# Weight tiles 576 bytes apart under moving rows 2112 bytes apart, 528 columns taken as 256 and 272, three raw buffers instead of four

## The chip, the core and the metric

The kernel runs on one core of one Trainium2 chip. The metric is the device time of one execution in microseconds, the median of the runs shown. Before the change three runs took 3562.27, 3562.84 and 3564.36 us.

## What is computed

The reference is a chain of two transformer-like blocks on one sequence of 512 tokens with 1024 features. The first block prepends 16 learned tokens (528 in all) and has two layers; each projects the normed sequence with one wide matrix, takes a sparse attention, a recurrent branch and a convolutional branch from it, merges the three through gates, and adds a gated feed-forward part:

```
for l in range(DEPTH):                      # 2 layers, T = 528
    n = rms_norm(h, mix_norm_g[l])
    proj = jnp.einsum("btd,de->bte", n, w_in[l])
    attn, rnn, cnv = ...                    # three branches of proj
    merged = g_attn * (attn @ w_o_attn[l]) + g_rnn * (rnn @ w_o_rnn[l]) + g_conv * (cnv @ w_o_conv[l])
    h = h + merged @ w_out[l]
    f = rms_norm(h, ffn_norm_g[l])
    h = h + (silu(f @ w_ffn_gate[l]) * (f @ w_ffn_up[l])) @ w_ffn_down[l]
return h[:, N_META:]                        # 512 tokens go on
```

The second block (feed-forward, neighbourhood attention beside a state-space branch, feed-forward, a gated product with a per-layer embedding, a last norm) works on the 512 tokens. All in float32. Most of the work is products of a float32 weight matrix with the sequence.

## The kernel before

**Three products for one.** A float32 product is made from float32r parts: a weight w is split into hi (its float32r rounding) and lo (the rest), the sequence likewise, and hi·xhi + hi·xlo + lo·xhi is summed in PSUM. The weights come from memory in 548 blocks of eight 128x128 tiles. SyncE loads block b into `raw[:, b % RAW]` (L475) once block b - RAW has been split. GpSimd splits it (`split`, from L488): L494 writes hi into `whi`, L496 writes lo into `wlo`. Each of these has two slots, and the split of block b waits until TensorE is done with block b - 2.

**Where the operands lie.** In a slot the eight weight tiles stand 512 bytes apart in each partition (128 columns of 4 bytes). The moving operand, the sequence, is kept with the features on partitions: `nhi`/`nlo`, `bhi`/`blo`, `ghi`/`glo`, `ahi`/`alo` are [128, k, 528], so their rows k are 2112 bytes apart; `nhi_s`, `ghi_s`, `ahi_s`, `zhi` and the like are [128, k, 512], with rows 2048 bytes apart. Layer 0 reads only the first sort. Layer 1 reads `nhi` and `bhi` (2112) in its projections and in the gates, often only 512 columns of each row from column 16 on, and the second sort elsewhere. After layer 1 all rows are 2048 apart. From the sizes in the code, `whi`, `wlo` and all of these tensors but `alo` start at the same remainder by 512; `alo` lies 384 bytes past it.

**The products.** `products` (L509) runs over the tiles of a block. With 512 columns a tile takes three matmuls (L521, L522, L524) into one PSUM bank. With 528 columns, which are more than a bank of 512 holds, a tile takes six: the columns are halved to 264 and 264, each half in a bank of its own (`acc[s][:, f, 0:TH]`), in the order hi·xhi, hi·xlo of the first half, the same of the second, lo·xhi of the first, lo·xhi of the second. Every matmul loads its 128x128 weights anew. `tile`, `part`, `parted_tile` and `first_tile` call it. Two accumulators `acc[0]` and `acc[1]` alternate; VectorE or ScalarE reads a finished one through `accv` (L425), whose view has the two halves as a dimension, so that the other operands of these instructions are halved too (`halves`).

**Down.** The last product of a feed-forward part has 22 row tiles, in three blocks: `cuts` makes them 7, 7 and 8.

The order on each engine is written out by hand, with semaphores between the engines; there is no scheduler.

Of the kernel before, what the change touches and what calls it, by code (L numbers as in the profile page):

```python
# [21 lines left out]
P = 128  # L22
# [24 lines left out]
RAW = 4  # L47
# [16 lines left out]
ITEMS = [[(hh, i) for hh in range(HEADS) for i in range(n)] for n in (NQT + 1, NQT)]  # L64
IX_TILE = 4
# [17 lines left out]
def cuts(nk, per):  # L83

    return [(c * nk // per, (c + 1) * nk // per - c * nk // per) for c in range(per)]
# [3 lines left out]
class Phase:  # L89
    def __init__(self, block, used, tiles, per, only):  # L90
        self.b0, self.used, self.tiles, self.per, self.only = block, tuple(used), tiles, per, only
# [9 lines left out]
    def nth(self, i):  # L101
# [17 lines left out]
      [("ple_products1", 1, 1, 2)] + [(f"ple_gate{i}", 1, 1, i % 2) for i in range(5, 8)]  # L119
PHASES = []  # L120
# [9 lines left out]
def plan():  # L130
    at, block, used = {}, 0, [0, 0, 0]
    for name, tiles, per, *only in PHASES:
        ph = at[name] = Phase(block, used, tiles, per, only[0] if only else None)
        block += tiles * per
        for i in range(tiles):
            used[ph.slot(i)] += 1
    return at, block
# [43 lines left out]
def build(nc, A_w, A_par, A_h, A_rope, A_gate, A_natab, A_namask, A_ssm, A_chunk, A_p, A_ident, A_out):  # L181
# [5 lines left out]
    with ExitStack() as ctx:  # L187
# [32 lines left out]
        whi = fixed("whi", [P, 2, BLK * P], F32R)  # L220
        wlo = fixed("wlo", [P, 2, BLK * P], F32R)
# [84 lines left out]
        alo, o = at("alo", [P, KF, T1], o, F32R)  # L306
# [11 lines left out]
        pap, o1 = at("pap", [P, 2, 8, 4, 32], (KF + PREP_FREE) * ROW)  # L318
# [106 lines left out]
        def accv(s, T):  # L425

            return halves(acc[s][:, 0, :], T) if T == 512 else acc[s][:, :, 0:T // 2]
# [57 lines left out]
        def _(pool):  # L485
            pool.wait_ge(sem("consts_set"), 3)

            def split(b, r, n):  # L488
                s = r % 2
                pool.wait_ge(sem(f"w_loaded{r}"), n)  # L490
                w = raw[:, r].rearrange("p (a c) -> p a c", a=BLK)
                hi = whi[:, s].rearrange("p (a c) -> p a c", a=BLK)
                lo = wlo[:, s].rearrange("p (a c) -> p a c", a=BLK)
# [3 lines left out]

            for b in range(NBLK):
                if b >= 2:
                    pool.wait_ge(pe_block, b - 1)  # L500
                split(b, b % RAW, 16 * (b // RAW + 1))
# [5 lines left out]
        def _(pe):  # L507
            def part(s, slot, j, rhs, T, a, z):

                return products(s, slot, j, 1, rhs, T, a, z, w0=j)  # L510
# [2251 lines left out]
```

## Time and profile before

| | |
|---|---|
| median of three runs | 3562.84 us |
| the profiled execution, its own time | 3565.33 us |
| its span | 3563.4 us |
| TensorE busy with matmuls | 3435.1 us, 96% |
| VectorE, ScalarE, GpSimd busy | 2382.9, 993.5, 2042.8 us |
| matmuls of 264 columns by `products`, 528-column tiles | 3200 of each: L521, L522, L524 |

A profile lists each instruction of one execution with its start, its duration and what it waited for. Matmuls overlap: the duration of one is longer than the time to the start of the next, so the pace of TensorE is read from starts, or from how many begin in a stretch. A stretch view gives for each stretch of the span the busy time of each engine with the number of its instructions in brackets, then the granted share of TensorE's clock (PEclk), the share of the DMA engines and their rate.

### The profile page before, as it was taken

The numbers are of one execution on the slowest core, as the hardware profiler recorded it, in microseconds if no ns is written. First come the engines' busy times: TensorE is split into PE (matmuls) and PEld (weight loads), VectorE is DVE, ScalarE is ACT, GpSimd is POOL, SyncE is SP. The second block draws the span as 40 slices with busy tenths as digits, with TensorE's granted clock in tenths as the row PEclk, the third lists the DMA queues.
The fourth block names the chain that finished last, engine by engine and source line by source line (L and its number), as shares of the span: only waits on it lengthen the run. The fifth ranks groups of instructions, "written<-read, shape, count | busy, mean of one in ns | idle before, by whom it ended". The sixth has DMA issues, their size and how long they took to land.

```text
span 3563.4 us, 49689 instructions
## 1 busy us (share of the span) xinstructions
PE 3435.1 (96%) x19988; PEld 2982.4 (84%) x19988; DVE 2382.9 (67%) x3005; ACT 993.5 (28%) x1716; POOL 2042.8 (57%) x1100
## 2 busy tenths in 40 slices
PE   7999899999999999999999999999999999999997
PEld 7899789999999879977778778878887875788886
DVE  6787898877833578888888863386336765743435
ACT  4406442312110241654232110111114444322201
POOL 4355334655766645533566766677665662466674
PEclk9999999999999999999999999999999999999998
DMA  3122111222323322211223432343335441223332
GB/s 137 60 89 78 48 48 66 83 89 96 126 89 100 111 68 89 81 55 56 83 86 106 147 127 101 100 147 127 100 104 203 142 154 52 91 94 100 101 106 71
DMA packets 96898, 348.29 MB, mean 98 GB/s; under 512 B 10848, under 2 KB 13152, under 8 KB 93664
## 3 DMA queue, kind: packets, MB, share of 16 engines
q1 hardware_dynamic: 80064, 289.44, 24.7%
q10 hardware_dynamic: 16672, 56.70, 4.2%
q8 instruction: 100, 1.64, 0.2%
q14 instruction: 62, 0.51, 0.0%
HBM read 322.32 MB, written 23.79 MB: 97 GB/s over the span
## 4 chain that ended last, share of the span: by engine, by line
PE 75%; DVE 18%; ACT 3%; issue 2%; DMA 1%; POOL 0%; ACTq 0%; DVEq 0%; POOLq 0%
PE acc L521 23%; PE acc L522 22%; PE acc L524 22%; DVE cu L2088 3%; PE acc L783 1%; PE aux L835 1%; DVE ptmp L2291 1%; PE acc L864 1%; PE aux L710 1%; DVE pap L2291 1%; DVE fpr L1821 1%; DVE mtmp L1875 1%; DVE pcp L2291 1%; PE aux L690 1%; PE aux L754 1%
## 5 line engine op out<-in xcount | busy, mean ns | idle before, releaser
L494 POOL TENSOR_SCALAR whi<-raw 128x1024 fp32r<-128x1024 f32 x548 | 624.9, 1140 | 1447.0 <-PE acc L524 1425.9
L496 POOL TENSOR_TENSOR wlo<-raw,whi 128x1024 fp32r<-128x1024 f32 x548 | 1418.0, 2588 | 45.7
L521 PE MATMUL acc<-nhi_s,whi 128*128 128x512 f32 x1568 | 619.8, 395 | 19.6 <-DVE fpr L1818 6.1
L524 PE MATMUL acc<-nhi_s,wlo 128*128 128x512 f32 x1568 | 612.0, 390 | 0.0
L522 PE MATMUL acc<-nlo_s,whi 128*128 128x512 f32 x1568 | 612.0, 390 | 0.0
L521 PE MATMUL acc<-bhi,whi 128*128 128x264 f32 (+1 forms) x1864 | 555.9, 314 | 12.3 <-ACT tqg L1149 5.5
L522 PE MATMUL acc<-blo,whi 128*128 128x264 f32 (+1 forms) x1864 | 542.0, 307 | 0.0
L524 PE MATMUL acc<-bhi,wlo 128*128 128x264 f32 (+1 forms) x1864 | 447.0, 306 | 0.0
L521 PEld LDWEIGHTS acc<-bhi,whi 128*128 128x128 f32 x1864 | 354.1, 190 | 43.4 <-issue 10.5
L521 PEld LDWEIGHTS acc<-nhi_s,whi 128*128 128x128 f32 x1568 | 295.3, 188 | 92.7 <-issue 13.5
L522 PEld LDWEIGHTS acc<-blo,whi 128*128 128x128 f32 x1864 | 353.8, 190 | 14.9
L524 PEld LDWEIGHTS acc<-nhi_s,wlo 128*128 128x128 f32 x1568 | 295.2, 188 | 61.8
L522 PEld LDWEIGHTS acc<-nlo_s,whi 128*128 128x128 f32 x1568 | 295.5, 188 | 60.5
L521 PE MATMUL acc<-nhi,whi 128*128 128x264 f32 x1208 | 326.6, 290 | 17.9 <-DVE nlo L1780 14.7
L522 PE MATMUL acc<-nlo,whi 128*128 128x264 f32 x1208 | 322.1, 287 | 0.0
L524 PEld LDWEIGHTS acc<-bhi,wlo 128*128 128x128 f32 x1864 | 303.8, 190 | 15.1
L524 PE MATMUL acc<-nhi,wlo 128*128 128x264 f32 x1208 | 247.7, 286 | 0.0
L521 PEld LDWEIGHTS acc<-nhi,whi 128*128 128x128 f32 x1208 | 228.3, 189 | 22.7 <-issue 14.2
L522 PEld LDWEIGHTS acc<-nlo,whi 128*128 128x128 f32 x1208 | 228.0, 189 | 1.6
L1818 DVE TENSOR_TENSOR fpr<-acc,frs 128x512 f32<-128x512 f32 (+1 forms) x88 | 61.2, 696 | 227.6 <-PE acc L524 222.7
L521 PE MATMUL acc<-ahi_s,whi 128*128 128x512 f32 x528 | 205.4, 389 | 0.0
L522 PE MATMUL acc<-alo_s,whi 128*128 128x512 f32 x528 | 205.4, 389 | 0.0
(410 smaller groups left out, 5865.1 us busy)
## 6 DMA issues: line engine op xcount, KB each, us to landing
raw<-in_w SPq DMA_DIRECT2D x548, 512.0 KB, 3.3
kept_cp<-pcp ACTq DMA_DIRECT2D x4, 1280.0 KB, 6.4
cp<-kept_cp ACTq DMA_DIRECT2D x4, 1280.0 KB, 10.2
kept_ap<-pap ACTq DMA_DIRECT2D x4, 1024.0 KB, 6.1
kept_cs<-pcs ACTq DMA_DIRECT2D x4, 1024.0 KB, 6.4
ap__151<-kept_ap ACTq DMA_DIRECT2D x4, 1024.0 KB, 6.9
cs__162<-kept_cs ACTq DMA_DIRECT2D x4, 1024.0 KB, 6.8
merge_gates<-gout ACTq DMA_DIRECT2D x16, 256.0 KB, 2.2
```

The source lines that it names most:

```text
L494: pool.tensor_scalar(hi, w, 1.0, 0.0, ALU.mult, ALU.add).then_inc(sem("w_hi"), 1)
L496: pool.tensor_tensor(lo, w, hi.bitcast(F32), ALU.subtract).then_inc(sem("w_split"), 1)
L521: pe.matmul(acc[s][:, f, 0:TH], hi, xh[:, f * TH:(f + 1) * TH], start=a, stop=False)
L522: pe.matmul(acc[s][:, f, 0:TH], hi, xl[:, f * TH:(f + 1) * TH], start=False, stop=False)
L524: m = pe.matmul(acc[s][:, f, 0:TH], lo, xh[:, f * TH:(f + 1) * TH], start=False, stop=z)
L690: m = pe.matmul(aux[z][:, 0, 0:cut], lhs, ki[rows, 0:cut], start=True, stop=True)
L710: m = pe.matmul(aux[g][:, f, 0:T1 // 2], rnn_w[:, g, n], ru[:, f * (T1 // 2):(f + 1) * (T1 // 2)], start=True, stop=True)
L754: m = pe.matmul(aux[0][0:r, 0, 0:min(W, 512)], lhs, k[:, hh // 4, 0:min(W, 512)], start=True, stop=True)
L783: m = pe.matmul(out, v[0:w, c, (hh // 4) * P:(hh // 4 + 1) * P], pts[0:w, c, 0:r], start=c == 0, stop=c == len(ps) - 1)
L1818: dve.tensor_tensor(halves(fpr[:, 0:T], T), accv(s1, T), rs, ALU.mult).then_inc(evac[s1], 1)
L2088: dve.scalar_tensor_tensor(y, x, w, total[z], ALU.mult, ALU.add).then_inc(sem("cv_conv"), 1)
L2291: tt = lambda o_, a, b_, op: then(dve.tensor_tensor(o_, a, b_, op))
```

## The change

1. `Phase.step` gives the distance of the weight tiles in a slot: 144 elements (576 bytes) for a block whose moving rows are 2112 bytes apart, 128 (512 bytes) for the others. GpSimd writes hi and lo at this distance, TensorE reads them there. The slots of `whi` and `wlo` grow to 1152 elements, and `raw` has three buffers instead of four.
2. 528 columns are taken as 256 and 272 instead of 264 and 264. The first 256 stand at the end of one PSUM bank and the other 272 at the start of the next, so that the accumulator is one run of 528, and `halves` goes from all instructions that read it.
3. `cuts` makes the three blocks of down 8, 8 and 6 tiles; `alo` moves by 128 bytes, to the same remainder by 512 as the others.

The core of the diff (in the functions that read an accumulator only `halves` goes; two of some twenty such places are shown):

```diff
-RAW = 4
+RAW = 3
+WSLOT = 144 * BLK
+CUT = 256
 def cuts(nk, per):
-    return [(c * nk // per, (c + 1) * nk // per - c * nk // per) for c in range(per)]
+    return [(c * BLK, min(BLK, nk - c * BLK)) for c in range(per)]
+    def step(self, i):
+        kind, l = self.name[:-1], self.name[-1]
+        if l == "0" and kind in FIRST_BLOCK:
+            return P + 16
+        if l == "1" and (kind in NORMED or kind in GATED and i % 2 == 0):
+            return P + 16
+        return P
+NORMED = ("vki", "qi", "kq", "conv", "rnn", "conv_gate")
+GATED = ("mg_rnn", "mg_att")
+FIRST_BLOCK = NORMED + GATED + ("conv_out", "out", "up", "down")
-        whi = fixed("whi", [P, 2, BLK * P], F32R)
-        wlo = fixed("wlo", [P, 2, BLK * P], F32R)
+        whi = fixed("whi", [P, 2, WSLOT], F32R)
+        wlo = fixed("wlo", [P, 2, WSLOT], F32R)
-        alo, o = at("alo", [P, KF, T1], o, F32R)
+        alo_place = o + 128
+        alo, o = at("alo", [P, KF, T1], alo_place, F32R)
         def accv(s, T):
-            return halves(acc[s][:, 0, :], T) if T == 512 else acc[s][:, :, 0:T // 2]
+            c = 0 if T == SEQ else CUT
+            return acc[s][:, :, :].rearrange("p a b -> p (a b)")[:, c:c + T]
-            def split(b, r, n):
-                s = r % 2
+            def split(b, r, n, step):
+                s = b % 2
-                hi = whi[:, s].rearrange("p (a c) -> p a c", a=BLK)
-                lo = wlo[:, s].rearrange("p (a c) -> p a c", a=BLK)
+                hi = whi[:, s, 0:BLK * step].rearrange("p (a c) -> p a c", a=BLK)[:, :, 0:P]
+                lo = wlo[:, s, 0:BLK * step].rearrange("p (a c) -> p a c", a=BLK)[:, :, 0:P]
-            def products(s, slot, j0, nk, rhs, T, first, last, w0=0):
-                TH = T // 2 if T > 512 else T
+            def products(s, slot, step, j0, nk, rhs, T, first, last, w0=0):
+                if T == SEQ:
+                    pieces = [(acc[s][:, 0, :], slice(0, SEQ))]
+                else:
+                    pieces = [(acc[s][:, 0, CUT:512], slice(0, 512 - CUT)), (acc[s][:, 1, 0:T - 512 + CUT], slice(512 - CUT, T))]
                 for j in range(nk):
-                    hi = whi[:, slot, (w0 + j) * P:(w0 + j + 1) * P]
-                    lo = wlo[:, slot, (w0 + j) * P:(w0 + j + 1) * P]
+                    hi = whi[:, slot, (w0 + j) * step:(w0 + j) * step + P]
+                    lo = wlo[:, slot, (w0 + j) * step:(w0 + j) * step + P]
-                    for f in range(T // TH):
-                        pe.matmul(acc[s][:, f, 0:TH], hi, xh[:, f * TH:(f + 1) * TH], start=a, stop=False)
-                        pe.matmul(acc[s][:, f, 0:TH], hi, xl[:, f * TH:(f + 1) * TH], start=False, stop=False)
-                    for f in range(T // TH):
-                        m = pe.matmul(acc[s][:, f, 0:TH], lo, xh[:, f * TH:(f + 1) * TH], start=False, stop=z)
+                    for out, c in pieces:
+                        pe.matmul(out, hi, xh[:, c], start=a, stop=False)
+                        pe.matmul(out, hi, xl[:, c], start=False, stop=False)
+                    for out, c in pieces:
+                        m = pe.matmul(out, lo, xh[:, c], start=False, stop=z)
-                    act.activation(halves(tqg[:, p % 2, 0:T], T), accv(s, T), ACT.Copy).then_inc(evac[s], 1)
+                    act.activation(tqg[:, p % 2, 0:T], accv(s, T), ACT.Copy).then_inc(evac[s], 1)
-                    dve.tensor_tensor(halves(fsl[:, 0:T], T), accv(s0, T), rs, ALU.mult).then_inc(evac[s0], 1)
+                    dve.tensor_tensor(fsl[:, 0:T], accv(s0, T), rs, ALU.mult).then_inc(evac[s0], 1)
```

No engine's instructions change their order. On TensorE the first tile of layer 0's down product stood in a row so before (`ahi`, `alo` are the moving operand, `whi`, `wlo` the weights, the size is that of the output):

```order
L521 MATMUL acc<-ahi,whi 128x264
L522 MATMUL acc<-alo,whi 128x264
L521 MATMUL acc<-ahi,whi 128x264
L522 MATMUL acc<-alo,whi 128x264
L524 MATMUL acc<-ahi,wlo 128x264 x2
```

and now:

```order
L541 MATMUL acc<-ahi,whi 128x256
L542 MATMUL acc<-alo,whi 128x256
L541 MATMUL acc<-ahi,whi 128x272
L542 MATMUL acc<-alo,whi 128x272
L544 MATMUL acc<-ahi,wlo 128x256
L544 MATMUL acc<-ahi,wlo 128x272
```

Six matmuls stay six, with the same 3 x 528 columns; only their sizes and addresses differ.

## Rows read from the trace of the kernel before

**Rows 1.** The page, part 1 and PEclk in 40 slices: busy us, share, instructions.
```profile
PE 3435.1 (96%) x19988; PEld 2982.4 (84%) x19988; DVE 2382.9 (67%) x3005; ACT 993.5 (28%) x1716; POOL 2042.8 (57%) x1100
PEclk9999999999999999999999999999999999999998
```
**Rows 2.** Timeline of PE in up of layer 0: start us, us, engine, line.
```profile
880.16 0.29 PE L521 MATMUL acc<-nhi,whi 128*128 128x264 f32 x1
880.28 0.29 PE L522 MATMUL acc<-nlo,whi 128*128 128x264 f32 x1
880.41 0.29 PE L521 MATMUL acc<-nhi,whi 128*128 128x264 f32 x1
880.53 0.29 PE L522 MATMUL acc<-nlo,whi 128*128 128x264 f32 x1
880.66 0.41 PE L524 MATMUL acc<-nhi,wlo 128*128 128x264 f32 x2
880.91 0.29 PE L521 MATMUL acc<-nhi,whi 128*128 128x264 f32 x1
...
881.64 0.29 PE L521 MATMUL acc<-nhi,whi 128*128 128x264 f32 x1
```
**Rows 3.** Stretches: conv and up (264), down (264), down and up (512), attention of layer 0.
```profile
190.00:280.00 90.00, 90.00 (x732) 89.74 (x730) 78.16 (x193) 8.30 (x13) 53.81 (x31) 1.00 0.26 88
840.00:1080.00 240.00, 239.41 (x1957) 239.20 (x1957) 155.03 (x190) 27.59 (x43) 154.85 (x83) 1.00 0.31 104
1084.00:1210.00 126.00, 126.00 (x1039) 125.84 (x1038) 39.92 (x33) 12.24 (x18) 81.33 (x47) 1.00 0.32 103
2192.00:2308.00 116.00, 115.85 (x512) 95.61 (x511) 39.47 (x33) 13.41 (x19) 80.01 (x47) 1.00 0.32 104
3140.00:3370.00 230.00, 230.00 (x1017) 190.50 (x1016) 89.61 (x85) 53.27 (x63) 153.02 (x85) 1.00 0.29 96
397.00:586.00 189.00, 174.22 (x1237) 155.55 (x1237) 178.40 (x318) 75.80 (x210) 67.87 (x33) 0.96 0.14 46
```
**Rows 4.** Timeline of PE in layer 1: first matmuls of three blocks of 24.
```profile
1723.76 0.40 PE L521 MATMUL acc<-bhi,whi 128*128 128x512 f32 x1
...
1729.34 0.40 PE L521 MATMUL acc<-nhi_s,whi 128*128 128x512 f32 x1
...
1734.79 0.40 PE L521 MATMUL acc<-bhi,whi 128*128 128x512 f32 x1
```
**Rows 5.** Groups of PE by form: count, busy us, mean ns, idle before.
```profile
L521 PE MATMUL acc<-bhi,whi 128*128 128x264 f32 x1520 | 413.2, 292 | 9.2 <-ACT tqg L1149 4.6 <-DVE blo L1880 2.1 <-DVE merged L2195 1.6
L521 PE MATMUL acc<-nhi,whi 128*128 128x264 f32 x1200 | 323.4, 289 | 17.9 <-DVE nlo L1780 14.7 <-ACT cgate L1293 2.2 <-DVE fpr L1818 0.6
L521 PE MATMUL acc<-bhi,whi 128*128 128x512 f32 x344 | 142.7, 415 | 3.1 <-DVE blo L1880 2.2 <-ACT tqg L1149 0.9
L521 PE MATMUL acc<-ahi,whi 128*128 128x264 f32 x352 | 92.4, 283 | 0.0
L521 PE MATMUL acc<-ghi,whi 128*128 128x264 f32 x128 | 34.0, 285 | 0.2 <-DVE glo L2166 0.2
```
**Rows 6.** Timeline of PEld: eight weight loads for matmuls of one column.
```profile
1327.99 0.98 PEld L627 LDWEIGHTS aux<-ones,tsq 128*128 128x128 f32 x8
```
**Rows 7.** Groups and waits of POOL, and waits of SP's queue.
```profile
L496 POOL TENSOR_TENSOR wlo<-raw,whi 128x1024 fp32r<-128x1024 f32 x548 | 1418.0, 2588 | 45.7
L494 POOL TENSOR_SCALAR whi<-raw 128x1024 fp32r<-128x1024 f32 x548 | 624.9, 1140 | 1447.0 <-PE acc L524 1425.9 <-PE aux L568 15.9 <-DMA raw<-in_w 5.1
SPq L475 <- POOL wlo L496: 3312.0, 542, 20.3
```
**Rows 8.** The page, part 6: DMA issues, KB each, median us to landing.
```profile
raw<-in_w SPq DMA_DIRECT2D x548, 512.0 KB, 3.3
```
**Rows 9.** Waits of PE for POOL: us in total, times, longest.
```profile
PE acc L521 <- POOL wlo L496: 3.5, 8, 1.0
```

More of the change, by code:

```diff
@@ L83, in cuts, with __init__ @@
 def cuts(nk, per):
-    return [(c * nk // per, (c + 1) * nk // per - c * nk // per) for c in range(per)]
+    return [(c * BLK, min(BLK, nk - c * BLK)) for c in range(per)]
 class Phase:
-    def __init__(self, block, used, tiles, per, only):
-        self.b0, self.used, self.tiles, self.per, self.only = block, tuple(used), tiles, per, only
+    def __init__(self, name, block, used, tiles, per, only):
+        self.name, self.b0, self.used, self.tiles, self.per, self.only = name, block, tuple(used), tiles, per, only
+    def step(self, i):
[5 more added lines that the diff above has]
+        return P
     def block(self, i):
@@ L132, in plan @@
     for name, tiles, per, *only in PHASES:
-        ph = at[name] = Phase(block, used, tiles, per, only[0] if only else None)
+        ph = at[name] = Phase(name, block, used, tiles, per, only[0] if only else None)
         block += tiles * per
@@ L496, in split @@
                 pool.tensor_tensor(lo, w, hi.bitcast(F32), ALU.subtract).then_inc(sem("w_split"), 1)
+            steps = [ph.step(i) for ph in AT.values() for i in range(ph.tiles) for _ in range(ph.per)]
             for b in range(NBLK):
@@ L537, in tile @@
                     if each is None:
-                        products(s, b % 2, k0, kk, rhs, T, c == 0, c == ph.per - 1).then_inc(pe_block, 1)
+                        products(s, b % 2, ph.step(i), k0, kk, rhs, T, c == 0, c == ph.per - 1).then_inc(pe_block, 1)
                         continue
@@ L542, in tile @@
                         pe.wait_ge(sem(ready), base + k0 + j + 1)
-                        p = products(s, b % 2, k0 + j, 1, rhs, T, c == 0 and j == 0, c == ph.per - 1 and j == kk - 1, w0=j)
+                        p = products(s, b % 2, ph.step(i), k0 + j, 1, rhs, T, c == 0 and j == 0, c == ph.per - 1 and j == kk - 1, w0=j)
                     p.then_inc(pe_block, 1)
@@ L601, in first_tile @@
                     pe.wait_ge(sem("norm_lo"), j + 1)
-                    p = part(s, b % 2, j, rhs, T1, j == 0, j == KD - 1)
+                    p = part(s, b % 2, ph.step(0), j, rhs, T1, j == 0, j == KD - 1)
                     if j == KD - 1:
@@ L796, in merge_part @@
                     for c in range(a, z):
-                        p = part(s, b % 2, c, rhs, T, c == 0, c == KD - 1)
+                        p = part(s, b % 2, mg.step(t), c, rhs, T, c == 0, c == KD - 1)
                     if z == KD:
@@ L853, in merge_part @@
                         pe.wait_ge(sem("z_lo"), c + 1)
-                    p = part(s, b % 2, c, R(zhi, zlo, S), S, c == 0, c == NQT - 1)
+                    p = part(s, b % 2, mg.step(t), c, R(zhi, zlo, S), S, c == 0, c == NQT - 1)
                     if c == NQT - 1:
@@ L1159, in proj @@
                         act.wait_ge(sem("qk_sum"), it - 1)
-                    act.activation(halves(tsq[:, e % 2, 0:T], T), accv(s, T), ACT.Square).then_inc(sem("qk_square"), 1)
+                    act.activation(tsq[:, e % 2, 0:T], accv(s, T), ACT.Square).then_inc(sem("qk_square"), 1)
                     act.wait_ge(sem("pj_done"), p - 1)
                     x, w = tqg[:, (5 + e) % 2, 0:T], tsw[:, (5 + e) % 2, 0:T]
-                    act.activation(halves(x, T), accv(s, T), ACT.Copy, scale=col("k_g" if e < KV else "q_g", l))\
+                    act.activation(x, accv(s, T), ACT.Copy, scale=col("k_g" if e < KV else "q_g", l))\
                        .then_inc(evac[s], 1)
@@ L1535, in projected @@
                     block_done(ph.b0 + 1)
-                    act.activation(halves(dst, S), accv(ph.slot(0), S), ACT.Copy, scale=HD2 ** -0.5 if i < 4 else 1.0)\
+                    act.activation(dst, accv(ph.slot(0), S), ACT.Copy, scale=HD2 ** -0.5 if i < 4 else 1.0)\
                        .then_inc(evac[ph.slot(0)], 1)
@@ L1809, in ffn @@
                 his, los = ffn_parts(T)
-                rs = halves(frs[:, 0:T], T)
+                rs = frs[:, 0:T]
                 def pair(m, hi, lo, work):
@@ L1847, in add_to_h @@
                     block_done(ph.block(n) + ph.per)
-                    hv = halves(h[:, n, T1 - T:T1], T)
+                    hv = h[:, n, T1 - T:T1]
                     if scale == 1.0:
```

46 lines of the change are left out of this document (23 added, 23 removed).

## The prediction

> **What bounds the kernel now.** I read the page's busy line first: TensorE has matmuls in flight for 96% of the span, at the granted clock of nine tenths or more in all slices but the last, and no other engine is above 67% [rows 1]. So the question is not who makes TensorE wait but how fast it goes while it does not. For that I read starts in a timeline [rows 2]: in up of layer 0 the six matmuls of a tile of 528 columns start about 0.12 us apart, and two tiles take 881.64 - 880.16 = 1.48 us, which is 123 ns for each matmul. The stretches say the same over many: 240 us / 1957 = 122.6 ns in up and 90 / 732 = 123 in conv; a count takes in one or two that overlap an edge, so I use 122.4. Down of layer 0 has 126 / 1039 = 121.3 [rows 3]. The clock granted in these stretches is 1.00, that is 2.4 GHz, at which 264 columns last 110 ns. Some 12 ns of each of these matmuls are therefore not columns.
>
> What could take them? The timeline of layer 1 has a comparison of its own [rows 4]: blocks of 24 matmuls of 512 columns that read `bhi` (rows 2112 bytes apart) alternate with blocks that read `nhi_s` (2048 apart), same instructions, same clock. The first takes 1729.34 - 1723.76 = 5.58 us, the second 5.45. Down on `ahi_s` has 116 / 512 = 226.6 ns, up 230 / 1017 = 226.2 [rows 3], and 5.58 / 24 is 232.5. So where the rows lie is worth 5.9 ns of 232.5, or 2.5%.
>
> Worked out from the code, the distance between a weight tile and its moving row modulo 256 bytes is always the same in the blocks of the second sort: per tile the row advances by 2048 and the weights by 512, together 1536, six times 256. In the first sort it shifts by 64 with each tile (2112 - 512 = 1600), and in 528-column tiles by another 32 at the second half (264 columns are 1056 bytes). That a constant distance is what makes the fast blocks fast is my reading: the weights stand 512 apart in both sorts, so the rows show an effect of the row distance, not yet one of the weights.
>
> **Part 1, weights at 576 and pieces of 256 and 272.** After the change a 2112 row meets weights 576 apart (2112 - 576 = 1536 again), and the second piece begins 1024 bytes on. So the distance stays constant in all six matmuls, except that the last of a tile runs while the weights of the next are loaded, 64 bytes further on.
>
> How much is it worth with short matmuls? No row has pieces this short with constant distance, so the price is bounded. As a ratio (5.45 / 5.58, -2.5%), 122.4 ns become 119.3; as the same 5.9 ns, 116.5. A floor is the weight load: eight loads for one-column matmuls last 0.98 us [rows 6], less one load's 0.19, over seven, 113 ns apart; so 116.5 is possible. From above, the fast 512-column blocks still spend 226.6 - 213.3 = 13.3 ns beyond their columns; if that is a fixed price of a matmul with a new weight load, pieces of 264 on average cost 123.3. I take the ratio, since the 12 ns of the short matmuls are fewer than the 19 of the slow long ones, so the loss seems to grow with the columns. And I take five sixths of it, for the one matmul in six whose next weights lie 64 off: 2.6 ns, down to 119.8.
>
> How many: 1520 + 1200 + 352 + 128 = 3200 of each of three lines, 9600 in all [rows 5]. In the attention stretch of layer 0 (397 to 586 us) VectorE is busy for 178.4 of 189 us [rows 3]; 16 blocks of 48 = 768 lie there, and I count nothing for them. Down's 1056 start from 121.3. The sum: 7776 x 2.6 = 20.2 us and 1056 x 1.5 = 1.6 us. The 344 tiles of 512 columns in 2112 rows are 43 blocks; 8 stand in attention again, and of the other 35 x 24 = 840 matmuls one in three has the 64 bytes, so two thirds of 5.9 ns: 3.3 us. Together 25.1 us. The gain lies on the path: GpSimd waits for TensorE, 1425.9 us in all [rows 7], not the other way (3.5 us, [rows 9]).
>
> The Trainium skill speaks against this change. The rows show 5.58 against 5.45 us for the same matmuls [rows 4]; "SBUF — State Buffer", section "Who interferes with whom", says that only VectorE's and GpSimd's shared ports cause contention and that TensorE never waits on anyone, with separate read ports for moving operand and weights. By that rule the sum of this part would be nothing; the rows differ from it as far as the row distance goes.
>
> **Part 2, three raw buffers.** A load now starts when block b - 3 is split instead of b - 4. A block lasts 48 x 122.4 ns = 5.9 us on TensorE and its split 1.14 + 2.59 = 3.73 us on GpSimd [rows 7], so from the end of one split to the start of the third next there are 3 x 5.9 - 3.73 = 13.9 us (before 19.8) for a landing of 3.3 us [rows 8]. With blocks of 5.45 us it is 12.6. SP's queue holds nothing else until the end, so nothing waits behind it. Cost nothing; a landing above 12 us would end that.
>
> **Part 3, GpSimd's writes in eight runs.** No row has them. Its cover is the wait of 5.8 - 3.73 = 2 us a block; below nothing they cannot help, since GpSimd is not waited for. Cost nothing, unless the split grows by more than half.
>
> **Part 4, down as 8, 8 and 6.** The short block lasts 18 x 226.6 = 4.08 us where the columns are 512. GpSimd's pair takes 80.0 / 23.5 = 3.4 us in that stretch [rows 3], so 0.7 us are left: nothing. If pairs took 4.4 us, 24 such blocks would cost 7 us.
>
> **Part 5, accumulators as one run.** Same elements, and no reader of an accumulator is waited for longer than the few us in [rows 5]: nothing.
>
> **The rivals.**
> - *The whole 5.9 ns are given back also to short matmuls.* For it: weight loads allow 113. Against: nothing shows it below 121. 7776 x 5.9 + 1056 x 4.8 + 840 x 5.9 + 768 x 5.9 = 60 us, 3502 us.
> - *The weights' distance does not matter*, only the rows' own addresses or nothing at all: the change does not do what it is for. For it: no row varies the weights' distance. 2112 rows still shift by 64 with each tile, and the time stays at about 3563 us. This is also where the rule of the skill named above ends.
> - *Slower: the constant state costs short pieces a fixed 13.3 ns each.* Then 256 columns take 106.7 + 13.3 = 120 and 272 take 126.7, 123.3 on average: 7776 x 0.9 + 1056 x 2.0 = 9 us more, 3572 us. It decides from an average of 122.4 up. For it: 226.6 is the least that 512 columns show. Against: the 264-column matmuls of today already spend less than that beyond their columns, in the bad state.
>
> **How the numbers follow.** The profiled run took 3565.33 us, 2.5 above the median; 3565.33 - 25.1 = 3540.2, and against the median 3562.84 - 25.1 = 3537.7, so 3538. Chances: the forecast 0.48, all of 5.9 ns 0.15, no effect 0.20, slower 0.17. A measurement here tells about 0.2% (7 us) from no change. Faster by more: 0.48 + 0.15 = 0.63; within: 0.20; slower: 0.17. The range goes from 3510 (most of the way to the first rival) to 3568 (no effect, with a part of the third).
>
> **What would show it.** In up of layer 0 a matmul should start every 119 to 120 ns (a block in 5.75 us), in layer 1 the blocks on `bhi` should come close to 5.45, and blocks on 2048 rows should not move. GpSimd should show no more waits for `raw` than today's one, and TensorE hardly more for `wlo`. Wrong is: 122 ns as before (second rival), 123 (third), or new waits of TensorE on GpSimd in down.

## The result, and the profile after

| | before | changed |
|---|---|---|
| median beside each other, nine runs each | 3563.02 us | 3570.8 us |
| their spread | 3560.43 to 3569.54 | 3570.06 to 3576.26 |
| the profiled execution, its span | 3565.33, 3563.4 us | 3570.07, 3568.1 us |
| ratio, 95% interval | | 1.0023 [1.0013, 1.0033] |

The change makes the kernel slower by 0.2%, 7.8 us, where 25 us of gain were forecast; the time lies above the range. The page of the changed kernel answers to [rows 1]: TensorE has more to do, not less, and no other engine has come near it.

```profile
PE 3439.0 (96%) x19988; PEld 2985.4 (84%) x19988; DVE 2385.5 (67%) x3005; ACT 993.5 (28%) x1716; POOL 2045.1 (57%) x1100
PEclk9999999999999999999999999999999999999999
```

The timeline of TensorE in up of layer 0, as in [rows 2] (start us, us, engine, line): 256 columns start some 0.12 us and 272 some 0.125 us after the one before. Two tiles take 881.22 - 879.74 = 1.48 us, the same 123 ns a matmul as before.

```profile
879.74 0.28 PE L541 MATMUL acc<-nhi,whi 128*128 128x256 f32 x1
879.86 0.28 PE L542 MATMUL acc<-nlo,whi 128*128 128x256 f32 x1
879.98 0.29 PE L541 MATMUL acc<-nhi,whi 128*128 128x272 f32 x1
880.11 0.29 PE L542 MATMUL acc<-nlo,whi 128*128 128x272 f32 x1
880.24 0.40 PE L544 MATMUL acc<-nhi,wlo 128*128 128x256 f32 x2
...
881.22 0.28 PE L541 MATMUL acc<-nhi,whi 128*128 128x256 f32 x1
```

The stretches say so over many matmuls. Columns as in [rows 3]: busy us of PE (count), PEld, DVE, ACT, POOL, then the granted clock, the DMA share and GB/s. In order they are conv and up (528 columns), down (528), down and up (512).

```profile
190.00:280.00 90.00, 90.00 (x731) 89.74 (x730) 78.08 (x193) 10.38 (x15) 52.16 (x31) 1.00 0.28 90
840.00:1080.00 240.00, 239.43 (x1954) 239.22 (x1954) 154.01 (x189) 25.84 (x40) 155.31 (x82) 1.00 0.30 102
1088.00:1212.00 124.00, 124.00 (x1011) 123.87 (x1010) 40.20 (x33) 10.95 (x16) 78.18 (x46) 1.00 0.33 111
2196.00:2312.00 116.00, 115.85 (x511) 95.59 (x510) 39.53 (x33) 13.40 (x19) 81.05 (x47) 1.00 0.31 105
3145.00:3375.00 230.00, 230.00 (x1016) 190.46 (x1015) 89.41 (x85) 52.68 (x63) 152.58 (x85) 1.00 0.28 96
```

Up holds 1954 matmuls where it held 1957, conv 731 for 732. Down has become slower: 124 / 1011 = 122.7 ns for 121.3. The stretches of 512 columns stand still. The parts that were costed at nothing did cost nothing. GpSimd's two instructions last what they lasted, and neither their wait for TensorE nor TensorE's for them has grown (groups and a wait, against [rows 7] and [rows 9]):

```profile
L510 POOL TENSOR_SCALAR whi<-raw 128x1024 fp32r<-128x1024 f32 x548 | 625.2, 1141 | 1449.4 <-PE acc L544 1428.1
L512 POOL TENSOR_TENSOR wlo<-raw,whi 128x1024 fp32r<-128x1024 f32 x548 | 1420.0, 2591 | 45.7
```

```profile
PE acc L541 <- POOL wlo L512: 3.6, 8, 1.0
```

Where the profiled pair differs can be read from the starts of the same matmul in both traces (difference of two starts after, less the same before; the order is the same, so every matmul has its counterpart):

| stretch, by its start before | us more after |
|---|---|
| up to the end of attention in layer 0, 586 | -2.9 |
| 528-column blocks up to down, 586 to 1083, up among them with +0.3 | +0.6 |
| down of layer 0 (127.86 us before) | +1.5 |
| start of layer 1 | +0.9 |
| its further projections, attention and gates | +0.2 |
| conv_gate of layer 1 (53.0 us before) | +2.3 |
| the next eight blocks | +1.6 |
| from there to 2931 | -0.4 |
| the products of the state-space branch (143.5 us before) | +1.1 |
| the rest | -0.1 |

The -2.9 us of the first stretch belong to that execution and not to the kernel: a kernel below (undo_gate) has the same instructions and addresses up to some 1800 us and stood at +0.7 there. Without it the sum of the rows, 7.7 us, is near the 7.8 us of the medians. A single row of one pair is less certain than that sum looks: from 586 to 1083 undo_gate, the same instructions again, loses 2.1 us where this pair shows 0.6.

### The profile page after: what moved, and what is told of

Same layout as the page of the kernel before. It is cut to its first block, busy times and chain, and to the rows that moved or that the text cites. A ratio compares the mean times of both kernels' runs of the same rounds, so it can differ in the third digit from the quotient of the medians.

```text
span 3568.1 us, 49689 instructions
## 1 busy us (share of the span) xinstructions
PE 3439.0 (96%) x19988; PEld 2985.4 (84%) x19988; DVE 2385.5 (67%) x3005; ACT 993.5 (28%) x1716; POOL 2045.1 (57%) x1100
## 4 chain that ended last, share of the span: by engine, by line
PE 75%; DVE 19%; ACT 3%; issue 2%; DMA 1%; POOL 0%; ACTq 0%; DVEq 0%; POOLq 0%
PE acc L541 23%; PE acc L544 22%; PE acc L542 22%; DVE cu L2108 3%; PE acc L803 1%; PE aux L855 1%; DVE ptmp L2311 1%; PE acc L884 1%; DVE fpr L1841 1%; DVE pap L2311 1%; PE aux L730 1%; DVE mtmp L1895 1%; DVE pcp L2311 1%; PE aux L710 1%; PE aux L774 1%
## 5 line engine op out<-in xcount | busy, mean ns | idle before, releaser
L510 POOL TENSOR_SCALAR whi<-raw 128x1024 fp32r<-128x1024 f32 x548 | 625.2, 1141 | 1449.4 <-PE acc L544 1428.1
L512 POOL TENSOR_TENSOR wlo<-raw,whi 128x1024 fp32r<-128x1024 f32 x548 | 1420.0, 2591 | 45.7
L541 PE MATMUL acc<-bhi,whi 128*128 128x256 f32 (+1 forms) x1864 | 555.3, 316 | 13.1 <-ACT tqg L1169 5.7
L542 PE MATMUL acc<-blo,whi 128*128 128x256 f32 (+1 forms) x1864 | 542.3, 306 | 0.0
L544 PE MATMUL acc<-bhi,wlo 128*128 128x256 f32 (+1 forms) x1864 | 447.2, 306 | 0.0
L541 PE MATMUL acc<-nhi,whi 128*128 128x256 f32 (+1 forms) x1208 | 325.4, 291 | 17.8 <-DVE nlo L1800 14.7
L542 PE MATMUL acc<-nlo,whi 128*128 128x256 f32 (+1 forms) x1208 | 323.5, 286 | 0.0
L544 PE MATMUL acc<-nhi,wlo 128*128 128x256 f32 (+1 forms) x1208 | 247.0, 285 | 0.0
L544 PE MATMUL acc<-ahi_s,wlo 128*128 128x512 f32 x528 | 205.4, 389 | 0.0
```

Of the source, the lines that this page charges most:

```text
L510: pool.tensor_scalar(hi, w, 1.0, 0.0, ALU.mult, ALU.add).then_inc(sem("w_hi"), 1)
L512: pool.tensor_tensor(lo, w, hi.bitcast(F32), ALU.subtract).then_inc(sem("w_split"), 1)
L541: pe.matmul(out, hi, xh[:, c], start=a, stop=False)
L542: pe.matmul(out, hi, xl[:, c], start=False, stop=False)
L544: m = pe.matmul(out, lo, xh[:, c], start=False, stop=z)
```

## The experiments

The expectations of the first four kernels set a constant distance of weights and rows against the rows' own places, and a fixed price of a short matmul against a proportional one.

**bench_pace: matmuls alone.** A kernel of its own: trains of matmuls in the kernel's order on eight tiles, with the distances of rows and weights, the first row's place, the lo part's place and the pieces set for each train. No other engine works beside them. Its core, with `W` the weights and `X` the rows in the kernel's own alignment:

```diff
+for c, (xs, ws, x0, lo, pieces, reps) in enumerate(CONFIGS):
...
+        for j in range(8):
+            wh, wl = ws * j, 1152 + ws * j
+            xh, xl = x0 + xs * j, x0 + lo + xs * j
...
+        m = pe.matmul(acc[c % 2][:, f, 0:n], W[:, w:w + P], X[:, x:x + n], start=start, stop=i == last[f])
```

> Left out: all of the reference's computation; 37 stretches of matmuls alone, each with its weight load, three to a tile as in the kernel (hi with xhi, hi with xlo, lo with xhi), 96 in a stretch (192 in the first and in those of two pieces), with the distances of rows and weights varied. Theory D, the distance between weight and row decides: rows 2048 with weights 512 takes 226.7 ns a matmul of 512 columns, 2112 with 512 takes 232 to 233, 2112 with 576 comes down to 227, and 2048 with 576 rises to 232. Theory R, the rows' own address modulo 256 decides and the weights' does not: 2112 stays at 231 to 233 with either distance of the weights, 2048 stays at 226.7 with either, 2304 (nine times 256) is at 226.7. For short pieces: theory F, a fixed price, columns plus 13.3 ns where the distance is constant, so 256 takes 120, 264 takes 123.3, 272 takes 126.7 and 320 takes 146.7; theory P, in proportion as the prediction had it, 256 takes 114 to 116, 272 takes 121 to 123.

Stretches, each from the first start of one setting to that of the next (columns as above, without ACT). In order: 512 columns with rows/weights 2048/512, 2112/512, 2112/576, 2048/576, 2304/512, 2304/576 apart; 2048/512 with all rows 64 and 128 bytes further on; one piece of 256, 264, 272 and 320 columns; 264+264 at 2112/512; 256+272 at 2112/576; 256+272 at 2304/512.

```profile
72.24:94.00 21.76, 21.76 (x97) 18.02 (x96) 0.69 (x1) 0.00 (x0) 1.00 0.00 1
94.00:116.25 22.25, 22.25 (x97) 18.03 (x96) 0.69 (x1) 0.00 (x0) 1.00 0.00 1
116.26:138.50 22.24, 22.24 (x98) 18.03 (x97) 0.69 (x1) 0.00 (x0) 1.00 0.00 1
138.50:160.73 22.23, 22.23 (x97) 18.05 (x96) 0.69 (x1) 0.00 (x0) 1.00 0.00 0
160.73:182.53 21.80, 21.80 (x97) 18.02 (x96) 0.69 (x1) 0.00 (x0) 1.00 0.00 1
182.53:204.76 22.23, 22.23 (x98) 18.03 (x97) 0.69 (x1) 0.00 (x0) 1.00 0.00 1
227.04:249.02 21.98, 21.98 (x97) 18.03 (x96) 0.69 (x1) 0.00 (x0) 1.00 0.00 0
249.03:271.34 22.31, 22.31 (x97) 18.09 (x96) 0.69 (x1) 0.00 (x0) 1.00 0.00 1
672.43:683.94 11.51, 11.51 (x98) 11.51 (x97) 0.69 (x1) 0.00 (x0) 1.00 0.01 2
683.94:695.47 11.53, 11.53 (x99) 11.53 (x97) 0.69 (x1) 0.00 (x0) 1.00 0.00 1
695.47:707.49 12.02, 12.02 (x98) 12.02 (x97) 0.69 (x1) 0.00 (x0) 1.00 0.01 1
720.13:734.21 14.08, 14.08 (x99) 14.08 (x98) 0.69 (x1) 0.00 (x0) 1.00 0.00 1
359.04:382.49 23.45, 23.45 (x193) 23.45 (x192) 0.69 (x1) 0.00 (x0) 1.00 0.01 1
382.49:406.01 23.52, 23.52 (x195) 23.52 (x194) 0.69 (x1) 0.00 (x0) 1.00 0.00 1
476.29:499.74 23.45, 23.45 (x194) 23.45 (x193) 0.69 (x1) 0.00 (x0) 1.00 0.00 1
```

A train is 96 matmuls, or 192 in two pieces (a count takes in up to three more, which overlap an edge). So 2048/512 takes 21.76 / 96 = 226.7 ns and 2112/512 takes 231.8. But 2112/576, where the distance is constant, takes 231.7 as well, and 2048/576, with the rows in their good places, has lost them too: 231.6. 2304/512, where rows and weights both stay at the remainder by 256 that they start at, gives 227.1 (226.7 in the second half of the train), 2304/576 does not, with 231.6; and rows and weights that stay, but with the rows 64 or 128 bytes past the weights' remainder, take 229.0 and 232.4. So for the good pace all starts have to lie at one remainder by 256 and remain there; whether a remainder other than this kernel's would do as well was not tried. The constant distance is refuted, and with it the view that only the rows count. Short pieces at 2304/512: 256 columns take 119.9 ns, 264 take 120.1, 272 take 125.2, 320 take 146.7. Beyond their columns (2.4 per ns, as the prediction counts them) that is 13.2 at 256 and 13.3 at 320, the 13.3 of 512, but 10.1 at 264 and 11.9 at 272: nearer to a fixed price than to one in proportion, though 448 columns spend 20.0. The two settings that matter, by the second half of each train: 122.36 before, 122.45 as changed. Alone, the change is worth nothing. And 256+272 take 122.2 even with all starts in place (2304/512): these two pieces have no good pace to come to.

**undo_step: weights 512 apart everywhere.**

```diff
     def step(self, i):
-        kind, l = self.name[:-1], self.name[-1]
-        if l == "0" and kind in FIRST_BLOCK:
-            return P + 16
-        if l == "1" and (kind in NORMED or kind in GATED and i % 2 == 0):
-            return P + 16
         return P
```

> The changed kernel with the weights 512 bytes apart in all blocks, the rest as changed. If the distance of the weights matters at all to pieces of 256 and 272 (theory D), the pace in up of layer 0 moves away from 122.6 ns and the time moves by over 7 us; if only the rows' addresses matter (theory R), the pace stays within 0.5 ns and the time stays within 0.1% of the changed kernel, 3568 to 3573 us.

3560.98 us beside 3564.55 of the kernel before: 0.9991 [0.9982, 1.0000]. Up holds x1965 (alone: 256+272 at 512 takes 121.8 ns). Without the wider distance the rest of the change is no loss: buffers, cuts, pieces and accumulators together do not slow it. The changed kernel has 1.0023, some 11 us more, so the weights' distance does matter in the kernel too, to its loss.

**undo_pieces: 264 and 264 again, as one run.**

```diff
-CUT = 256
+CUT = 512 - 264
```

> The changed kernel with 528 columns taken as 264 and 264 in one run over two banks, the rest as changed. If the unequal pieces cost something (the 272 one is bound by its columns, the 256 one by its weight load), this is faster than the changed kernel by 3 to 9 us; if the price is fixed for each matmul, the same within 2 us.

3565.36 us: 1.0004 [0.9995, 1.0013], up x1964 (alone 121.95). Against the changed kernel's 1.0023 that is some 7 us less, the first of the two expectations: with weights 576 apart the unequal pieces cost something. The pace is 0.5 x 8832 = 4.4 us of it.

**undo_down: alo and the blocks of down as before.**

```diff
-    return [(c * BLK, min(BLK, nk - c * BLK)) for c in range(per)]
+    return [(c * nk // per, (c + 1) * nk // per - c * nk // per) for c in range(per)]
-        alo_place = o + 128
+        alo_place = o
```

> The changed kernel with down in blocks of 7, 7 and 8 tiles and alo where it was. Down of layer 0 went from 127.9 to 129.3 us in the two traces. If alo's place (128 off modulo 256) was what made down faster than up before, this gives back 1.5 us there and nothing else; if the three blocks cost a wait in each down product, up to 5 us; if neither matters, 3570 us as changed.

3571.7 us: 1.0019 [1.0010, 1.0028], up x1955. The time does not come back. Nor does down's pace, which was the first expectation: from the first matmul of down in layer 0 to the first behind it 128.94 us pass, where the kernel before has 127.86 and the changed one 129.33. Of the 1.47 us, 0.39 come back.

**bench_place: where the parts may lie.** The same trains with more to set.

```diff
-for c, (xs, ws, x0, lo, pieces, reps) in enumerate(CONFIGS):
+for c, (xs, ws, x0, lo, wl, pieces, order, reps) in enumerate(CONFIGS):
...
+        for kind, f in order:
+            bank, at, o, n = pieces[f]
+            w, x = ((wh, xh), (wh, xl), (wx, xh))[kind]
```

> Computes nothing of the reference: trains of matmuls from fixed data, no other engine beside them (two warm-ups and 39 settings). Questions: where may the pieces, the rows' lo part and the weights' lo part lie, and in which order may the six matmuls stand, so that 264+264 columns go faster than 122.4 ns? Address theory (every operand's start modulo 256 counts, its own and its neighbours' in the order): a lo part 128 bytes off gives 121.1 again, other offsets something between 120 and 122.5, and a second piece that starts at 1280 bytes in rows of 2560 (all starts multiples of 256) gives 120.0, as one piece of 264 had. Rival (two pieces and two banks cost by themselves): that setting stays at 122. For the remainder of the changed kernel: 256 and 272 with the first at the end of its bank, weights 576 apart, should be 122.45 if the place in the bank does not matter; if it is 122.8 or more, the accumulator as one run costs 3 us or more in all.

Stretches of 192 matmuls at rows 2112 and weights 512 apart if not said otherwise: the setting of before; lo rows 128 bytes off; rows of 2560 bytes with the second piece at 1280; the changed kernel's own places in the banks (2112/576); the three products of the first piece ahead of the three of the second.

```profile
141.73:165.22 23.49, 23.49 (x194) 23.49 (x193) 0.69 (x1) 0.00 (x0) 1.00 0.01 1
235.28:258.51 23.23, 23.23 (x194) 23.23 (x193) 0.69 (x1) 0.00 (x0) 1.00 0.01 1
539.14:562.18 23.04, 23.04 (x195) 23.04 (x193) 0.69 (x1) 0.00 (x0) 1.00 0.00 1
585.51:609.03 23.52, 23.52 (x195) 23.52 (x193) 0.69 (x1) 0.00 (x0) 1.00 0.00 1
702.79:725.99 23.20, 23.20 (x195) 23.20 (x193) 0.69 (x1) 0.00 (x0) 1.00 0.01 1
```

23.49 / 192 = 122.3 ns before. With all starts a multiple of 256 apart it is 23.04 / 192 = 120.0, in two banks as one piece in one bank. A lo part 128 bytes off gives 121.0, which is the pace of down before the change, whose `alo` lay 128 bytes off modulo 256 (121.3 in [rows 3]). The accumulator as one run costs TensorE nothing (122.5, as with the pieces at the start of each bank). And the order alone gives 120.8.

**undo_gate: only conv_gate of layer 1 back at 512.** This one tests where 2.3 us of the table come from.

```diff
-NORMED = ("vki", "qi", "kq", "conv", "rnn", "conv_gate")
+NORMED = ("vki", "qi", "kq", "conv", "rnn")
-FIRST_BLOCK = NORMED + GATED + ("conv_out", "out", "up", "down")
+FIRST_BLOCK = NORMED + GATED + ("conv_gate", "conv_out", "out", "up", "down")
```

> The changed kernel with only the eight blocks of conv_gate in layer 1 back at weights 512 apart. Collision theory: blocks on bhi at weights 576 are 0.028 us shorter, so GpSimd's split starts some 0.1 us earlier against VectorE's chain of cstat, one more of VectorE's additions lies under a split and lasts 2.1 us longer, and TensorE waits 4.5 us instead of 2.3 for cstat and then runs at the lower clock for a while. With 512 the wait should be 2.3 again, the blocks 5.58, and the time 3567 (2.3 less than the changed kernel) to 3566. Rival (the wait differs from run to run by itself): the wait stays at 4.5 or comes out anywhere, and the time stays at 3570.8. Second rival (GpSimd's writes at 576 are what slows VectorE): the same as the collision here, but then GpSimd's or VectorE's instructions under a split should be longer at 576 in other places too, which the groups would show.

3567.06 us beside 3561.81: 1.0012 [1.0003, 1.0021], where the changed kernel has 1.0023; the two intervals overlap, so the times alone do not settle it. The wait does, in the kernel before, the changed one and undo_gate (us in all, times, longest):

```profile
PE aux L726 <- DVE cstat L2144: 2.3, 1, 2.3
```

```profile
PE aux L746 <- DVE cstat L2164: 4.5, 1, 4.5
```

```profile
PE aux L746 <- DVE cstat L2164: 2.3, 1, 2.3
```

GpSimd's and VectorE's timelines at that place show the cause (start us, us, engine, line, what ended the idle time). Before:

```profile
1818.90 1.57 POOL L494 TENSOR_SCALAR whi<-raw 128x1024 fp32r<-128x1024 f32 x1 [1.28 <-PE acc L524]
1820.56 2.66 POOL L496 TENSOR_TENSOR wlo<-raw,whi 128x1024 fp32r<-128x1024 f32 x1
```

```profile
1812.63 0.68 DVE L2144 TENSOR_TENSOR cstat<-cstat,csq 128x512 f32<-128x512 f32 x1
...
1818.09 2.92 DVE L2144 TENSOR_TENSOR cstat<-cstat,csq 128x512 f32<-128x512 f32 x3
```

and changed:

```profile
1818.89 1.05 POOL L510 TENSOR_SCALAR whi<-raw 128x1024 fp32r<-128x1024 f32 x1 [1.18 <-PE acc L544]
1820.03 2.65 POOL L512 TENSOR_TENSOR wlo<-raw,whi 128x1024 fp32r<-128x1024 f32 x1
```

```profile
1818.19 5.04 DVE L2164 TENSOR_TENSOR cstat<-cstat,csq 128x512 f32<-128x512 f32 x3
```

```profile
1820.58 2.64 DVE L2164 TENSOR_TENSOR cstat<-cstat,csq 128x512 f32<-128x512 f32 x1
```

The line of 5.04 us is three additions, and the last line is the third of them by itself. One such addition takes 0.68 us by itself. Against VectorE's chain the split came 0.1 us earlier: 0.70 us after the last group of additions began, where it was 0.81. That sufficed for the hi write to get through first (1.05 us for 1.57). The lo write began 0.53 us earlier, and the last addition stood behind it: it took 2.64 us, and the three together 5.04 for 2.92. TensorE waits 4.5 us for the result. The kernels below and above bear it out: where the split starts at most 0.76 us after the first of the three additions (undo_pieces, undo_down, lo128, order_after, best) the wait is 4.5 us as well, and where it starts 0.79 us after it or later (undo_step, only_pieces, order) it is 2.2 or 2.3. The 0.1 us come from the gain itself: the split starts when a block ends, and blocks on `bhi` take 1729.61 - 1724.06 = 5.55 us now for the 5.58 of [rows 4], so three of them are 0.09 us ahead.

**only_pieces: the kernel before with 256 and 272 and the accumulator as one run.** The instructions that read an accumulator lose their `halves` as in the change.

```diff
+CUT = 256
-            return halves(acc[s][:, 0, :], T) if T == 512 else acc[s][:, :, 0:T // 2]
+            c = 0 if T == SEQ else CUT
+            return acc[s][:, :, :].rearrange("p a b -> p (a b)")[:, c:c + T]
-                TH = T // 2 if T > 512 else T
+                    pieces = [(acc[s][:, 0, CUT:512], slice(0, 512 - CUT)), (acc[s][:, 1, 0:T - 512 + CUT], slice(512 - CUT, T))]
```

> The kernel before with 256 and 272 columns and the accumulator as one run, nothing else: four raw buffers, weights 512 apart, alo and the blocks of down where they were. By the pace measured alone (121.8 for 122.36 ns): 8544 x 0.56 = 4.8 us less than the kernel before, 3558, or 0.9987. If the accumulator as one run costs its readers something, it is above that: 3563 and more. If three raw buffers cost something, then this is faster than undo_step (3561.0) by more than the 0.7 us that alo explains.

3562.27 us: 1.0000 [0.9990, 1.0009]. Up has x1966, the pace that was expected; of the 4.8 us the profiled execution shows 2.6 at the end, the median nothing.

**lo128: the kernel before with the lo parts 128 bytes off.**

```diff
-RAW = 4
+RAW = 3
+        place[0] += 128
         nlo = fixed("nlo", [P, KD, T1], F32R)
+        place[0] += 384
-        blo, o = at("blo", [P, KD, T1], o, F32R)
+        blo, o = at("blo", [P, KD, T1], o + 128, F32R)
+        o += 384
-        glo, _ = at("glo", [P, KD, T1], 0, F32R)
+        glo, _ = at("glo", [P, KD, T1], 128, F32R)
```

> The kernel before with nlo, blo and glo placed 128 bytes past their hi parts modulo 512, as alo has always been (and three raw buffers, for the room). Address theory: the 264-column matmuls go from 122.36 to 121.1 ns as they do in down and alone; 7776 x 1.26 = 9.8 us less, 3553, or 0.9972; up of layer 0 should hold x1977 in its 240 us. Rival (what counts in down is something else, its longer rows of blocks): x1957 as before and 3563. A collision of GpSimd with VectorE can take 2 to 4 us of it back.

3560.84 us: 0.9999 [0.9990, 1.0008], although up has x1976. The pace came, the time did not: at 1800 us the profiled execution was 6.5 us ahead of the kernel before; conv_gate of layer 1 then took 2.3 us back with the same wait of 4.5 us, and the next blocks 1.6.

**bench_order: places and distances with the new order.** The same kernel with other settings, nearly all in this order:

```diff
-((0, 0), (1, 0), (0, 1), (1, 1), (2, 0), (2, 1))
+((0, 0), (1, 0), (2, 0), (0, 1), (1, 1), (2, 1))
```

> Computes nothing of the reference: trains of matmuls from fixed data as in bench_place, two warm-ups and 40 settings, nearly all with the three products of the first piece ahead of the three of the second. If the order works by itself, 264+264 and 256+272 are both near 120.8 at weights 512 apart, and weights at 576 and a lo part elsewhere move it by under 0.5 ns. If it works by the starts of neighbours modulo 256, as the other order does, the settings spread by 1 ns or more, and some with a shifted lo part lie below 120.8; none lies below 120.0, which is what all starts on multiples of 256 give.

Three of its settings: 264+264 at weights 576 with the lo parts 224 bytes off, 256+272 as in the changed kernel, and 264+264 with all starts in place (rows of 2560 bytes, weights 512 apart).

```profile
375.45:398.55 23.10, 23.10 (x195) 23.10 (x194) 0.69 (x1) 0.00 (x0) 1.00 0.01 1
538.56:562.08 23.52, 23.52 (x195) 23.52 (x194) 0.69 (x1) 0.00 (x0) 1.00 0.00 1
772.40:795.69 23.29, 23.29 (x195) 23.29 (x193) 0.69 (x1) 0.00 (x0) 1.00 0.00 1
```

Between 120.3 and 123.6 ns everything occurs; 23.10 / 192 = 120.3 is the best, the changed kernel's places stay at 122.5. No setting that fits the kernel reaches the 120.0. The last line shows that starts are not all there is: the places that give 120.0 in the old order give 23.29 / 192 = 121.3 in the new one. Why is open.

**order: the kernel before, one line less.**

```diff
                         pe.matmul(acc[s][:, f, 0:TH], hi, xl[:, f * TH:(f + 1) * TH], start=False, stop=False)
-                    for f in range(T // TH):
                         m = pe.matmul(acc[s][:, f, 0:TH], lo, xh[:, f * TH:(f + 1) * TH], start=False, stop=z)
```

> The kernel before with one line less: the three products of the first 264 columns come before the three of the second (hi.xhi, hi.xlo, lo.xhi, then again), where the old order had both hi pairs and then both lo.xhi. Address theory: 120.83 ns for 122.36 alone; 7776 x 1.53 = 11.9 us less, and some 0.3 x 1056 in down; 3563 becomes 3550 to 3552, or 0.9965. Up of layer 0 should hold x1983 in its 240 us (122.7 ns to 121.1 by the same count). Rival (a second load of the same lo weights or a change of bank costs more in the kernel than alone): x1957 or less and 3563. The phases of GpSimd against VectorE can move it by 2 to 4 us either way.

3555.65 us beside 3563.05: 0.9980 [0.9971, 0.9989]. Faster than both kernels, though by 7.4 us and not by the 11 to 13 expected. Its stretch of up:

```profile
840.00:1080.00 240.00, 239.32 (x1980) 239.10 (x1978) 150.72 (x186) 25.23 (x39) 156.71 (x83) 1.00 0.31 105
```

**order_after: the same line out of the changed kernel.**

> The changed kernel with the same line taken out. If the weights' distance and the 256 and 272 columns are worth something of their own once the order is grouped, this is faster than order by more than 2 us; if they are worth nothing, it lies 2 to 8 us above order as the changed kernel lies above the kernel before (3571 against 3563); 3551 to 3559.

3573.55 us: 1.0029 [1.0018, 1.0041], up x1955. A miss: it stays where the changed kernel is, 18 us above order, as bench_order's 122.5 has it. An order is good only for the places that it meets.

**best: bench_order's best setting in the kernel.** The diff is against the changed kernel:

```diff
-CUT = 256
+CUT = 512 - 264
-        if l == "1" and (kind in NORMED or kind in GATED and i % 2 == 0):
+        if l == "1" and kind in NORMED:
+        place[0] += 224
         nlo = fixed("nlo", [P, KD, T1], F32R)
-        alo_place = o + 128
+        alo_place = o + 96
-                    for out, c in pieces:
                         m = pe.matmul(out, lo, xh[:, c], start=False, stop=z)
...
```

`blo` and `glo` are moved by 224 bytes as `nlo` is, and conv_gate goes back to 512 in layer 1 as in undo_gate.

> The best setting of bench_order put into the kernel: weights 576 apart under 528-column tiles (512 apart again for the layer-1 tiles of 512 columns in conv_gate and the gates), 264 and 264 columns, the three products of a piece together, and nlo, blo, glo, alo 224 bytes past their hi parts modulo 256. Alone it takes 120.27 ns for the 122.36 of the kernel before and the 120.83 of order. Address theory: 7776 x 2.09 + 1056 x 0.8 = 17 us less than the kernel before, of which phases of GpSimd against VectorE take 2 to 5 back as they did in order: 3548 to 3552, and up of layer 0 holds x1988 to x1992 in its 240 us. Rival (a pace found alone on eight tiles does not carry over where VectorE and GpSimd write at the same time): up holds x1980 or fewer, and the time is that of order, 3556, or more.

3555.22 us beside 3563.94: 0.9976 [0.9964, 0.9987]. Up has its pace:

```profile
840.00:1080.00 240.00, 239.30 (x1988) 239.03 (x1987) 151.41 (x180) 26.51 (x41) 158.68 (x84) 1.00 0.31 104
```

but hardly more time saved than by order: 13.9 us ahead at 1560 us, it gives 2.3 back in conv_gate by the 4.5 us wait and 1.6 in the next blocks. The 3548 to 3552 us that were expected are missed.

**Pace alone and pace in the kernel.** Up's count in 240 us, and the one that follows from the matmuls alone as 1957 x 122.36 / ns:

| kernel | alone, ns | expected | counted | time / before |
|---|---|---|---|---|
| before | 122.36 | | 1957 | 1 |
| order_after | 122.50 | 1955 | 1955 | 1.0029 |
| changed | 122.45 | 1956 | 1954 | 1.0023 |
| undo_pieces | 121.95 | 1964 | 1964 | 1.0004 |
| undo_step, only_pieces | 121.80 | 1966 | 1965, 1966 | 0.9991, 1.0000 |
| lo128 | 121.10 | 1977 | 1976 | 0.9999 |
| order | 120.83 | 1982 | 1980 | 0.9980 |
| best | 120.27 | 1991 | 1988 | 0.9976 |

## Why the prediction failed

**The bound was right.** TensorE's pace sets the time, and a count in up follows the matmuls alone to 3 in 1990 without any other engine.

**The reading that failed** is the one that the prediction called its own: "That a constant distance is what makes the fast blocks fast". [rows 4] do show an effect of the rows' places, and alone it is 231.8 for 226.7 ns. But nothing in them tells a constant distance from operands that all stay at one remainder by 256, since in the fast blocks both hold. 2112/576 and 2304/576 told them apart: the 576 throws away what it should have restored. So 2.6 ns became -0.1 (122.36 to 122.45 alone), and 7776 x 2.6 = 20.2 us became 7776 x 0.1, a loss of 0.8. The five sixths went with it; the counts of 9600 and 7776 are as they were.

**The price of the pieces** failed on its own. The sum put 256 and 272 columns in the good state at 119.8 ns; alone, with all starts in place, they take 122.2. So a distance that had worked would have been worth 0.2 ns as long as 528 was cut there, and 264 and 264 with all starts in place take 120.0. The ratio was taken because the loss "seems to grow with the columns": in the good state 256, 320 and 512 columns all spend 13.2 or 13.3 ns beyond their columns, so that reason does not hold. (The ratio itself is a little large: 5.45 / 5.58 is 2.3% less, not 2.5%.)

**Down had the wrong sign.** It was to gain 1.5 ns for each of 1056 matmuls and lost 1.4: 1.5 us in the traces. The prediction saw that `alo` lies 384 bytes past the others and that down is faster, and did not put the two together. Alone, lo rows 128 bytes off are the whole difference, 121.1 for 122.36; the change moved `alo` away from there. But undo_down shows that in the changed kernel this place alone brings back only 0.39 us. Step by step down of layer 0 takes 127.86 us before, 128.25 with the new pieces (only_pieces), 128.59 with `alo` and the blocks of down changed too (undo_step) and 129.33 with weights 576 apart: the wider distance is half of the loss.

**The 512-column tiles on 2112 rows** were to give 3.9 ns each and gave (5.58 - 5.55) / 24 = 1.2; bench_place, with the rows 64 bytes on as there, has 231.8 and 230.6 ns for weights 512 and 576 apart.

**Parts 2 to 5** hold: no new wait for `raw`, 3.6 us of waits for `wlo` for 3.5, 1141 and 2591 ns for GpSimd's instructions, and undo_step, which keeps all of them but the writes of Part 3, is not slower than before. What the argument for Part 3 left out is that GpSimd can cost without being waited for: VectorE is, and it stands behind GpSimd's write.

**The rivals.** That the weights' distance does not matter had 0.20 and a time of 3563. It was right that 2112 rows stay slow with weights 576 apart, and wrong in its reason: the distance does matter, 2048 rows lose their pace by it, and undo_step gains some 11 us without it. The slower one had the time, 3572, by luck for the most part, as its reason explains little of it: 256 columns do take 120, but the average of a tile came out at 122.45, not 123.3, and the pace is worth 0.8 us in the long blocks and 1.5 in down, 2.3 of its 9. The rest of the 7.8 us came from elsewhere: 2.3 us are the collision in conv_gate, shown by the wait in undo_gate. The 1.6 us in the next blocks are stretches at the lower level of TensorE's clock. 0.6 of them follow the 4.5 us wait itself: TensorE is back at its full pace 5.6 us after that wait, in the kernel before 3.7 us after its wait of 2.3. The other 1.0 is this stretch in the changed kernel:

```profile
1845.80:1849.30 3.50, 3.50 (x10) 2.73 (x9) 2.50 (x1) 0.01 (x1) 1.95 (x1) 0.51 0.16 47
```

A granted 0.51 is 1.2 of 2.4 GHz; it began after a wait of 1.8 us for `cgate`. undo_gate and only_pieces, which do not have the collision, lose the same 1.0 us there after the same wait of 1.8 us; undo_step waited 2.0 us for `cgate` and kept its clock. The 1.1 us in the state-space branch have the same look, matmuls that start 427 ns apart. There the kernel before runs at the lower level too, for a shorter time: between 2930 and 2990 us it is granted 0.94, the changed one 0.91. Why one execution loses the clock and another does not stays open, and so does how much of the last 2 us belongs to the change. lo128 and only_pieces, whose pace is worth 10 and 5 us and whose medians show 1 and none, are not fully accounted for either.

**The rule named in the prediction** would have given 3563: the Trainium skill, "SBUF — State Buffer", section "Who interferes with whom", has TensorE wait for no other engine. The bench does not speak against it: no other engine worked while 226.7 became 231.7 ns. The exclusive lock that the same section of the Trainium skill puts on the ports which VectorE and GpSimd share fits the addition of 2.64 us beside a write of 2.65. A second sentence does not help to understand the rows: the Trainium skill's "TensorE: Matmul & The Clock Gate", section "Step-by-step: what each phase is for", says that loading the next weights takes no read bandwidth from the running matmul; with the rows unchanged, weights 576 for 512 bytes apart cost 5 ns of 226.7. Whether that is bandwidth or something else the runs do not show.

## What to carry to other kernels

Where a row shows that a place in memory matters, two explanations that agree in all existing rows (a distance that stays, remainders that are equal and stay) need matmuls timed alone before a layout is built on one of them. Try the order of the matmuls first: one line gave 120.8 for 122.4 ns without moving a byte, though only with the places that it met: in the changed kernel the same line gave nothing. And ask of each gain which other engines' work it shifts: 0.03 us a block put one VectorE addition behind GpSimd's write and cost TensorE 2.2 us.

## What the runs showed of the hardware

- A float32r matmul of 512 columns with fresh weights takes 226.7 ns if all rows and weights start at one remainder by 256, and 228.9 to 233.3 in the other settings tried, whichever operand moves (second half of each train, here and in the next two lines).
- With all starts in place, 256 and 264 columns both take 120.0 ns, 272 take 125.4; 128, 192 and 224 all take 111.7, so there the columns do not set the pace. That the weight loads do is likely, as they are 113 ns apart in [rows 6], but was not tested.
- In two pieces of 264 the mean goes from 120.0 to 123.6 ns with the places and the order of the operands alone.
- An addition on VectorE that takes 0.68 us takes 2.64 when it meets GpSimd's write of 2.65 us.
